# Dilated stage: seven units of the z projection moved out of the projection, padded keys written by the rotary step

## The reference

```
q, k, v, z = split(h @ w_in, 4)                  # h: 512 x 1024, w_in: 1024 x 4096
q, k = rope(q), rope(k)                          # 16 heads of 64
for each query block, head group gi of 3 (6, 5, 5 heads; patterns (128,1), (512,4), (2048,16)):
    s = q . k[kpos] * scale                      # kpos = tq - dil * arange(win // dil + 1), where >= 0
    m = max(s); e = exp(s - m); den = sum(e); outs[gi] = (e / den) @ v[kpos]
    lses[gi] = logsumexp(m + log(den), over the group's heads) - log(heads)
alpha = softmax(lses over groups) * 3            # a weight for each token and group
y = (concat(outs[gi] * alpha[gi]) * silu(z)) @ w_out
```

## Time and profile before

| | us |
|---|---|
| median of three runs | 2256.88 |
| the profiled execution | 2260.57 |
| its span, from the first to the last instruction | 2258.7 |
| projection stage of the dilated mixer, first to last unit | 451.4 to 629.5 |
| attention of the dilated mixer, first scores to last product | 634.3 to 689.0 |
| group weights and mixing, to the first matmul of the output projection | 689.0 to 706.5 |

### The profile page before, as it was taken

The page is one execution under the profiler, slowest core; times in us unless marked ns, Lnnn a source line. Parts: engine busy times, 40 slices in busy tenths (PEclk is TensorE's granted clock), DMA queues, the critical chain, the costliest instruction groups (busy, mean ns, idle before and its releaser), DMA issues.

```text
span 2258.7 us, 32281 instructions
## 1 busy us (share of the span) xinstructions
PE 2193.4 (97%) x11943; PEld 1965.8 (87%) x11943; DVE 1573.1 (70%) x3027; ACT 924.0 (41%) x1510; POOL 1247.0 (55%) x670
## 2 busy tenths in 40 slices
PE   7999999999989999999999999999999999999999
PEld 6898899888888878888999999999998888888887
DVE  6736867574466656442899999999983787666665
ACT  3235566332264423531334334555553333333332
POOL 1634222355412341233488788766656888787875
PEclk9999979999999999999999999999999999999999
DMA  7253414222501242124478888999989999999995
GB/s 282 85 186 105 148 62 136 90 95 94 168 1 58 100 146 88 61 81 140 137 238 285 278 286 271 342 354 338 346 292 346 351 370 355 365 351 360 350 359 218
DMA packets 164476, 492.43 MB, mean 218 GB/s; under 512 B 15072, under 2 KB 64608, under 8 KB 162912
## 3 DMA queue, kind: packets, MB, share of 16 engines
q1 hardware_dynamic: 107872, 305.79, 39.2%
q0 software_dynamic: 36864, 134.23, 16.0%
q10 hardware_dynamic: 19584, 50.34, 5.8%
HBM read 437.87 MB, written 52.43 MB: 217 GB/s over the span
## 4 chain that ended last, share of the span: by engine, by line
PE 40%; DVE 8%; POOL 2%; DMA 1%; issue 0%; ACT 0%; DVEq 0%; SPq 0%; ACTq 0%
PE ps L2379 23%; PE ps L2343 13%; PE ps L2361 4%; POOL t_split L2488 1%; DVE arena L2607 1%; DVE arena L2576 1%; DVE arena L2567 1%; DVE arena L2568 1%; DVE rope L2545 1%; DVE norm_rows L2545 1%; DVE arena L2602 1%; DVE arena L2572 1%; DVE arena L2563 1%; DVE arena L2545 0%; DVE arena L2610 0%
## 5 line engine op out<-in xcount | busy, mean ns | idle before, releaser
L2488 POOL TENSOR_TENSOR t_split<-t_raw,t_split 128x1024 fp32r<-128x1024 f32 x225 | 551.9, 2454 | 211.5 <-ACT t_split L2414 209.4
L2343 PE MATMUL ps<-h_hi,t_split 128*128 128x384 f32 x2048 | 536.8, 338 | 8.1 <-POOL t_split L2488 5.1
L262 POOL TENSOR_TENSOR w_split<-ring,w_split 128x1024 fp32r<-128x1024 f32 x113 | 272.2, 2409 | 493.0 <-ACT w_split L254 447.2
L2379 PE MATMUL ps<-t_split,w_split 128*128 128x512 f32 x2304 | 523.1, 390 | 1.5 <-DVE w_split L2657 1.5
L2379 PEld LDWEIGHTS ps<-t_split,w_split 128*128 128x128 f32 x2304 | 432.4, 188 | 92.1 <-DVE w_split L2657 2.2
L286 PE MATMUL ps<-h_hi,w_split 128*128 128x512 f32 x1440 | 452.5, 392 | 0.0
L2414 ACT ACTIVATE t_split<-t_raw 128x1024 fp32r<-128x1024 f32 x256 | 270.4, 1057 | 344.0 <-PE ps L2379 243.5
L2343 PEld LDWEIGHTS ps<-h_hi,t_split 128*128 128x128 f32 x2048 | 372.7, 189 | 10.8 <-POOL t_split L2488 7.3
L2343 PE MATMUL ps<-h_lo,t_split 128*128 128x384 f32 x1024 | 343.8, 336 | 0.0
L286 PEld LDWEIGHTS ps<-h_hi,w_split 128*128 128x128 f32 x1440 | 270.4, 188 | 56.6 <-issue 0.7
L286 PE MATMUL ps<-h_lo,w_split 128*128 128x512 f32 x720 | 280.5, 390 | 0.0
(11 more groups left out here) (341 smaller groups left out, 3201.4 us busy)
## 6 DMA issues: line engine op xcount, KB each, us to landing
ring<-w_stream SPq DMA_DIRECT2D x203, 512.0 KB, 3.3
t_raw<-u_table SPq DMA_DIRECT2D x128, 512.0 KB, 4.6
t_raw<-v_table SPq DMA_DIRECT2D x128, 512.0 KB, 6.1
gelu_scratch<-e_gel ACTq DMA_DIRECT2D x128, 192.0 KB, 4.9
gates_scratch<-arena ACTq DMA_DIRECT2D x8, 3072.0 KB, 13.3
arena<-gelu_scratch SPq DMA_DIRECT2D x32, 768.0 KB, 5.9
arena<-gates_scratch SPq DMA_DIRECT2D x32, 768.0 KB, 9.0
first<-w_stream SPq DMA_DIRECT2D x16, 512.0 KB, 13.4
```

The source lines that it names most:

```text
L262: pool.tensor_tensor(w_split[:, i % RS, 1, :], ring[:, n % R, :], w_split[:, i % RS, 0, :].bitcast(F32), ALU.subtract).then_inc(lo_done, 1)
L2343: mm = pe.matmul(ps[:, 6 + n % 2, 0:NT], t_split[:, n % RAWS, u, k * P:(k + 1) * P], h_parts[h][:, k, P:T], start=(k + u + h == 0), stop=( ...
L2379: mm = pe.matmul(ps[:, 2 * i + half, :], w_split[:, b % 2, w, at:at + P], t_split[:, m % RAWS, v, half * 512:(half + 1) * 512], start=(n + ...
L2488: pool.tensor_tensor(t_split[:, m % RAWS, 1, :], t_raw[:, m % RAWS, :], t_split[:, m % RAWS, 0, :].bitcast(F32), ALU.subtract).then_inc(t_ ...
```

## The change

- **z units.** The projection stage ends with unit 24. Units 25 to 30 run in the attention: in steps n = 0 to 59, eight of every ten steps take the three matmuls of one k, into bank 7, between the transposes and the product with the values. ACT copies each out after its eighth step, and splits the weights of units 27 to 31 and of the first output piece on the way; POOL splits their low parts. Unit 31 runs in the group weights' stage in place of the first `keep_busy`: 18 of its matmuls ahead of the permutation matmuls, 6 behind them. z is now copied plainly, and Silu is applied in the group weights' stage, by ACT, one unit at a time.
- **Keys.** `kd_pad` moves out of the place of `h_hi`/`h_lo`, which must live on. The rotary step of a key unit writes its two heads straight to `kd_pad`, with two additions of 64 partitions instead of one of 128. The zeros are written by eight memsets of POOL (128 x 1024) in the projection stage, behind the cosine of units 4 to 11. The copies at the start of the attention go.
- **Modulation and sine arguments.** The pieces of chunk 8 stand in the stream behind units 9, 11, 13 and 15, and DVE multiplies two of them after each of r = 7, 9, 11, 13. The first half of the sine chain (10 instructions) stands in DVE's list behind r = 2, the second (8) behind r = 4. PE's `ada_chunk` runs at u = 22.

Memory is laid out anew; the attention's output goes to the place of `qd`. The diff, cut (the layout of `area`s, the `attention` signature and `width` are left out):

```diff
-ADA6, ADA9, ADA12 = range(27, 31), (4, 5, 6, 7, 12, 13, 14, 15), (7, 8, 9, 10)
+ADA6, ADA9, ADA12 = (9, 11, 13, 15), (4, 5, 6, 7, 12, 13, 14, 15), (7, 8, 9, 10)
...
+                if r < roped.whole:
+                    dve.tensor_tensor(dst(r), order(r, t1[:, r % 2, :]), order(r, ps[:, 4 + r % 2, :]),
+                                      ALU.add).then_inc(roped.done.sem, 1)
+                else:
+                    for half in range(2):
+                        at = slice(half * DH, (half + 1) * DH)
+                        dve.tensor_tensor(dst(r, half), order(r, t1[at, r % 2, :]), order(r, ps[at, 4 + r % 2, :]),
+                                          ALU.add).then_inc(roped.done.sem, 1)
...
-                ask_pieces(sp, units6[-1] + 1 + R)
+                ask_pieces(sp, units6[Z_FIRST] + 1 + R)
...
-                for u in range(2, 32):
+                for u in range(2, Z_FIRST + 1):
...
-                rope_dil[3].wait(pe, 16)
-                ada_chunk(pe, 8, ada_sum6, 4)
+                    if u == 22:
+                        rope_dil[3].wait(pe, 16)
+                        ada_chunk(pe, 8, ada_sum6, 4)
...
-                for u in range(32):
-                    if u + 3 < 32:
+                for u in range(Z_FIRST + 1):
+                    if u + 3 < Z_FIRST + 3:
                         split_hi(act, units6[u + 3])
...
-                        ins = act.activation(zd[:, u - 24, :], b, ACT.Silu)
+                        rope_dil[3].wait(act, 16)
+                        ins = act.activation(zd[:, u - Z_FIRST, :], b, ACT.Copy)
...
-                for u in range(2, 32):
+                for u in range(2, Z_FIRST + 3):
                     split_lo(pool, units6[u])
                     if 3 <= u < 19:
                         rope_dil[1](pool, u - 3)
+                    if 4 <= u < 12:
+                        half, at = (u - 4) % 2, (u - 4) // 2 * 2
+                        pool.memset(kd_pad[:, half, at:at + 2], 0.0).then_inc(pad_zeroed.sem, 1)
...
+                for r in range(16):
+                    if r >= 8 and r % 2 == 0:
+                        pad_zeroed.wait(dve, r - 6)
+                    rope_dil[2](dve, r)
+                    if r == 2:
+                        sine_arguments(0, 0.25)
+                    elif r == 4:
+                        sine_arguments(1, 0.0)
+                    elif r in (7, 9, 11, 13):
+                        for j in range(r - 7, r - 5):
+                            ada_piece(dve, 8 * KD + j, ada_sum6)
...
+        def dil_pe_filler(pe, n):
+            u, k = z_turn(n)
+            if u >= Z_LAST or k >= KD:
+                return
+            if k == 0:
+                z_weights[u] = piece_ready(pe, units6[u])
+                if u > Z_FIRST + 1:
+                    left6(pe, u - 1)
+            for a, b in HI_LO:
+                mm = pe.matmul(ps[:, 7, :], z_weights[u][:, a, k * P:(k + 1) * P], h_parts[b][:, k, :],
+                               start=(k + a + b == 0), stop=(k == KD - 1 and a == 1))
+            if k == KD - 1:
+                mm.then_inc(piece_used, 1)
+
+        dil_splits = {2: units6[27], 12: units6[28], 22: units6[29], 32: units6[30], 42: units6[31], 52: out_f}
...
-                for g in (1, 2):
+
+                def gated(u):
+                    act.activation(zd[:, u, :], zd[:, u, :], ACT.Silu).then_inc(f_silu.sem, 1)
...
+                gated(0)
+                diagonals(1)
+                act.wait_ge(piece_used, used_of(units6[Z_LAST] + 1))
+                act.activation(zd[:, KD - 1, :], ps[:, 3, :], ACT.Silu).then_inc(ev6["act"].sem, 1)
+                gated(1)
+                diagonals(2)
+                gated(2)
+                split_hi(act, PIECES["dil_out"][2])
                 for u in range(KD):
+                    if u + 3 < KD - 1:
+                        gated(u + 3)
                     act.wait_ge(f_z, u + 1)
                     act.activation(h_hi[:, u, :], zd[:, u, :], ACT.Copy).then_inc(f_hi, 1)
...
             def pe8(pe):
-                keep_busy(pe, 4, 12)
...
+                last_gate(range(6))
                 pe.wait_ge(f_y, 1)
...
+                last_gate(range(6, KD)).then_inc(piece_used, 1)
+                keep_busy(pe, 4, 6)
```

133 lines of the change are left out of this document (81 added, 52 removed).

## The result

Five runs of the changed kernel took 2274.3 to 2280.65 us, median 2278.66; five of the kernel before have the median 2261.59. The ratio on record is 1.0093, 95% interval 1.0068 to 1.0118, which is 15 to 27 us: **slower by 17 us** by the two medians (a ratio of 1.0075), where +11 was forecast. In a control, the changed kernel run once more later, the ratio was 1.0077 (1.0053 to 1.0101) and the medians 16.5 us apart. The direction and the places were right; the size of the stalls between the rotary steps was not.

A forecast was written before the change was run, and what follows sets the result against it. PE, busy for 97% of the span, was taken to bound the kernel. Parts 1 to 3 (-12.7 us) and part 4 (+23.4) gave +10.7 on 2260.6, or 2271.3; less 3.7 to the median, 2267.6, say 2268; range 2245 to 2279.

The forecast's parts named there:

- Parts 1 to 3: Projection stage's end, attention and group weights through mixing: together -12.7 us.
- Part 1: Seven units leave the projection stage; unit 24's end to first scores falls from 42.71 to 3.2 us: -39.5 us.
- Part 2: Six units enter the attention, partly filling idle or half-clock PE time: +24.9 us, attention 79.6, bounds 77 and 84.
- part 3: Unit 31 and Silu in group weights: +1.9 us; permutation matmul +1.4 at clock 0.60, -0.2 if it holds; mixing +0.5.
- Part 4: Work pushed between rotary steps: DVE's SBUF-only instructions take turns with POOL and stall PE, +23.4 us.
- sine chains: Behind r = 2 and r = 4, chains wait out POOL's instructions; units 7 and 9 stall 6.8 us each.
- ring's loop: Pair, request, landing, split, copy, rotary step loop: 14.3 us per two units; stalls 1.5, 3.4, 3.4, 1.5 at units 12 to 17/18.
- From there 3.3 us to land: In the weight ring, a unit's weights land 3.3 us after the request; with 4.0 us, part 4 would be 26.
- The half clock: PE's clock after a projection-stage stall lies beside DVE, which is last; otherwise part 4 would be 26 to 30 us.
- The forecast's own case: Whole kernel: slower, 2262 to 2275 around 2268 us, chance 0.50.
- half of the work hides: Rival on DVE's added work between rotary steps: part 4 at 8 to 18 us, no change, 2252 to 2262; chance 0.20.
- the prediction's other figure for part 4: Between rotary steps: if the sine chains' six multiply-adds do not wait for memsets, 22 us instead of 23.4.

The follow-up runs named there:

- The kernel with both moves: Changed kernel with sine chains and modulation pairs behind the v copies, column sums behind unit 24: 2249.3 us beside 2260.3 for the kernel before.
- the chains in PSUM: Changed kernel with the sine chains' intermediate values in two idle PSUM banks, same place and instruction count: 2264.5 us beside 2260.3 before.
- quarter loads: Changed kernel with the dilated stage's eight modulation pieces loaded for 32 of 128 partitions: 2275.8 us beside 2257.9 before; again, 2271.2 beside 2258.6.
- the three pairs above: Modulation pairs meeting a memset in the changed kernel with POOL's memsets behind units 10 to 17 instead of 4 to 11: 2278.5 us beside 2259.8 before.
- the kernel with the pairs moved: Changed kernel with modulation pairs behind v copies 0 to 3 and column sums behind unit 24: 2263.2 us beside 2260.3 before.

## Why the prediction came out as it did

**Parts 1 to 3, -12.7 forecast:** right, within 2 us. The kernel with both moves has them alone: 2249.3 against 2260.3 is -11.0, and anchor to attention's end is 223.79 against 237.59, -13.8 where parts 1 and 2 had -14.6. Part 1 came to 0.2 us. Part 2 was 1.8 us short, 0.04 per filled step, inside its bounds. In part 3 the term for the clock was right, though this profile doesn't show it: here the permutation matmul came 4.2 us into its block at a clock of 1.00, the bound of -0.2. So it did in three of the thirteen traces with z units. In the other ten, the control and the kernel with both moved among them, the clock was 0.71 to 0.74 in that stretch, the matmul came 5.6 to 5.8 us in, and the first mixing matmul 10.8 to 11.0 us behind the attention against 9.57 before, the +1.4 of the forecast. So the z matmuls, which all of them have, are not what held it, and no run shows what did. The mixing lost 1.5 instead of 0.5 in all thirteen; here its last eight instructions waited 1.2 us for DVE L1860.

**Part 4, +23.4 forecast, +28.8 measured** (26.8 in the control). These 5.4 us are most of the 6.5 by which the sum of the stretches was missed (17.2 against 10.7). One by one, the delay of a unit's start against the kernel before (there 5.44 us a unit, counted back from the first transposes, 98.05 behind the anchor) grew by:

| | forecast | measured |
|---|---|---|
| unit 7 | 6.8 | 5.0 |
| unit 9 | 6.8 | 6.1 |
| unit 12 | 1.5 | 5.0 |
| unit 14 | 3.4 | 4.4 |
| unit 16 | 3.4 | 6.3 |
| unit 17, first transposes | 1.5 | 2.0 |

The **sine chains** were right in kind and 2.5 us too dear: 15.4 instead of 17.2 and 8.9 instead of 9.8, though the seven instructions of POOL were in the way as foreseen. I had added POOL's time and the chain's own; most of the waiting instructions' own time lies inside POOL's (12.5 us beside POOL and 2.9 behind it, for the first chain). The prediction also called some 30 us of added work for DVE a fit where DVE had 27 to spare. That was no fit: in the ring's part DVE was booked for 13.5 us where PE takes 10.9, and with the chains in PSUM their bare work still cost 7.7.

The **ring's loop** was right in kind and 7.9 us too cheap (6.1 in the control), and the step that failed is one number: "From there 3.3 us to land". That is the median of a stream in which one piece is asked for at a time; the landings took 6.4, 4.9 and 6.4 us, beyond even the 4.0 of the prediction's bound. I did not follow my own sentence on SyncE to its end: a pair that frees two places lets four pieces be asked for, and the unit is behind the next pair. Three landings later by 3.1, 1.6 and 3.1 us are 7.8; in the control 2.8, 1.2 and 2.5 are 6.4. With quarter loads the loop took 14.2 to 14.8 us, the 14.3 of the prediction, and the ring's part came to 10.9 and 11.9 where the forecast had 9.8. That the 28.8 lie between the prediction's 26 and 30 for "half clock" is luck: that bound was for another reason.

**The half clock**, of which the prediction said that it would "lie beside DVE", did so where it was tested, behind the stops before units 7 and 16. In the trace 11.1 of the 30.7 us look like lost clock (30.7 less 17.7 of idle and 1.84 of column sums), but giving them back at units 7 and 16 gave idle instead.

**The rivals.** The forecast's own case held, with the sum of 10.7 coming out at 17.2. That half of the work hides was wrong in both of its forms: the second chain met a POOL that was idle for a while and still cost 6.1, and the stalls built up no slack for the ring.

**The memsets.** The six multiply-adds of the chains would not have waited for a memset, by the three pairs above, so the prediction's other figure for part 4, 22 instead of 23.4, had the better ground, and its sentence that an SBUF-only instruction of DVE "does not run beside one of POOL" was too wide. It makes the forecast no better. What stays open is the price of the memsets in time.

## What to carry to other kernels

Free time of an engine is not free time at its memory port: before small SBUF-only instructions of DVE are put into a stage where POOL works without pause, price a dependent chain at about the length of POOL's queue beside it and then what is left of its own (here 12.5 and 2.9 us), or send its operands through idle PSUM; and add up DVE's own work against the room it has. In a ring of few places, list what each release lets be asked for and where in that burst the urgent piece stands. Work that is moved off the critical engine must be placed where nobody's next input hangs on the engine that takes it: here the same instructions cost 29 us between the rotary steps and, but for 1 us of column sums, nothing behind the v copies.

## What the runs showed of the hardware

- A DVE instruction that waits for POOL does not always get the next turn. L1640 started inside a cosine, which ended at 474.18, and ended at 475.35, 0.3 us after the memset that followed it: two of POOL's instructions went ahead of it. L1645 did the same 4.9 us later, and both did in the control. It made no difference to the sum, for both of POOL's instructions were in the queue.
- A DVE multiply-add with two SBUF inputs and a POOL memset ran at the same time (1.08 us behind the cosine beside a memset, 1.07 without one), where a DVE instruction with one SBUF input waited for a memset to end.
- The ACT table load between the exponential and Silu, in the group weights:

```profile
705.94 0.20 ACT L1774 ACTIVATE ps<-arena 128x24 f32<-128x24 f32 x1 [4.75 <-DVE arena L1840]
706.16 1.28 ACT L1777 ACT_TABLE_LOAD   x1
707.45 0.63 ACT L1777 ACTIVATE arena<-arena 128x512 f32<-128x512 f32 x1
```

  1.31 us from the end of one to the start of the other. The Trainium skill, ScalarE: Activation LUTs, section What ACT_TABLE_LOAD costs, adds a drain of about 1.38 us; by that, an estimate, Silu would have started at 708.8. This row, like the earlier trace rows, shows no drain.
- A stop of the same length did not always bring the clock down. Behind 3.22 us before unit 9 the changed kernel ran at 0.50 to 0.53 for some six us; behind 3.40 us in the kernel with the pairs moved it stayed at 1.00 (windows: stretch, length, PE busy, PEclk, DMA share, GB/s):

```profile
510.00:512.00 2.00, 0.00 (x0) 1.00 0.25 102
512.00:514.00 2.00, 0.82 (x4) 1.00 0.00 0
514.00:516.00 2.00, 2.00 (x10) 1.00 0.00 0
```
